# Memory keys and values moved into the MLP, and the norms and first blocks of the second stage cut into token halves

## The chip, the cores and the metric

The kernel runs on one core of a Trainium2 chip. The metric is the device time of one execution in microseconds (us); smaller is better. Matrix products run on TensorE (PE), elementwise work on VectorE (DVE) and ScalarE (ACT), small fills on GpSimd (POOL), and SyncE (SP) issues the transfers. Each engine works through its own list of instructions strictly in order, and waits on semaphores for what the others have made.

## The reference

One sequence of 1,024 tokens, 1,024 features, goes through two stages. The first is a residual block with a gated long convolution, a recurrent branch, a mix of both, and an MLP:

```
h = rms_norm(x, g_mlp); f = square(relu(h @ w_1)); x = x + f @ w_2
return rms_norm(x, g_final)
```

The second stage normalises that result again, projects it, and adds three branches to it. Of them the change touches the beginning of two and the memory's side of the third:

```
mn = rmsnorm(mem, mem_norm_g); km, vm = split(mn @ w_kv)     # 256 memory rows
u -> sums over windows of 2, 4, 8, 16 tokens -> pool_w -> gate by zb
gates (8 columns) -> log-sigmoid, cumulative sum, cumulative maximum over the tokens
```

All is float32 in the reference.

## The kernel before, in words

**Products.** Every float32 operand of a large product is split into a high part and a low part, so that one product becomes three matmuls (`three_products`, L564 to L566). Activations lie feature-major, as 8 tiles of 128 features by 1,024 tokens; a weight block of 1,024 by 128 against one half of the tokens (512) is 8 x 3 = 24 matmuls, and a whole block has two such halves (`block`, `block_product`).

**Weights.** All weight blocks stand in one list, `blocks`, and pass through two raw buffers and three split buffers. SP loads block i once block i-2 has been split (`ahead`, L423); ACT makes the high part (L946) and DVE the low part (L1471), both once PE has used block i-3. Where in its list each engine does this is written out by hand, by calls of `ahead(k)`.

**PSUM.** Results go to banks that are handed out in a ring (`Rota`, L107). In the MLP the ring has six banks: who asks for a bank waits until the sixth request before it has been read out and freed. At the second stage the ring grows to eight.

**The end of the MLP.** The MLP runs in four quarters (f = 0 to 3). Of each, eight blocks `w1` make a quarter of f, and eight blocks `w2` are added to x (L1832). In the last quarter each finished tile of x is squared by ACT (`stat_square`, L1186), and DVE adds it into two running sums (L1799, L1800): one of the squares and one of the squares times the squared gain, from which both norms, one after the other, are computed. Memory is loaded and normalised there too.

**After the MLP.** PE turns the normalised memory feature-major (L749), DVE and ACT split it (L955, L1486), and four key blocks (24 matmuls of 256 columns) and four value blocks (12 matmuls of 512 columns) follow. Within them PE sums the running sums over the features by one-column matmuls (L730), DVE computes both norms' factors (L1870 to L1882), PE spreads the factors over the partitions (L605), and h3, the input of the second stage, is scaled by DVE (L1861) and split by ACT and DVE (L955, L1483). Then `y1_start` (L1890) makes x into the first norm's result, 16 instructions.

**The second stage's start.** Blocks `gates`, then for each of four groups `u`, `zb` and `pw`, then the four blocks `ob`. DVE computes on the gate rows (4 partitions by 1,024 tokens) cumulative sums (L1896 to L1905) and maxima (L1906 to L1919); PE transposes one of these rows (L791). For each group DVE sums windows over u (L1949 to L1958), ACT and DVE split the result, `pw` multiplies it, and it is gated (L1922, L1975). `ob` needs all four groups.

Of the kernel before, what the change touches and what calls it, by code (L numbers as in the profile page):

```python
# [9 lines left out]
P = 128  # L10
# [109 lines left out]
def build_program(nc, A, out):  # L120
    ctx = ExitStack()
    with ctx:
# [102 lines left out]
        for j in range(DT):  # L225
            need(("wo", j), w_o, 0, DT, j * P, P)
        for f in range(FC):
            for j in range(DT):
                need(("w1", f, j), w_1, 0, DT, (f * DT + j) * P, P)
            for j in range(DT):  # L230
                need(("w2", f, j), w_2, f * D, DT, j * P, P)
        for c in range(NH):
            need(("kv", c), w_kv, 0, DT, c * P, P)
        for c in range(NH):
            need(("kv", NH + c), w_kv, c * 2 * P, 2, GROUP, GROUP)
# [3 lines left out]
        for g in range(NH):  # L239
            need(("u", g), w_in2, 0, DT, Y_U + g * P, P)  # L240
            need(("zb", g), w_in2, 0, DT, Y_ZB + g * P, P)
            need(("pw", g), A["pool_w_2"][0, g], 0, 1, 0, P)
# [99 lines left out]
        sqm = [sb(f"sqm{n}", "g", 36 * KB + 4096 * n, [P, SEQ]) for n in range(2)]  # L342
        square_sum = [sb(f"square_sum{n}", "g", 44 * KB + 4096 * n, [P, SEQ]) for n in range(2)]
        tmp2 = [sb(f"tmp_2_{n}", "g", 72 * KB + 2048 * n, [P, HALF]) for n in range(4)]
# [4 lines left out]
        row = [sb(f"row{n}", "g", (8 + 17 + 8) * KB + 4096 * n, [P, SEQ]) for n in range(5)]  # L349
# [66 lines left out]
        def sync(sp):  # L416
# [81 lines left out]
            ahead(number["kv", 2 * NH - 1] + 2)  # L498
# [4 lines left out]
            ahead(number["gates"] + 2)  # L503
# [8 lines left out]
            sp.dma_start(rcnt[:], A["rcnt"]).then_inc(*landed("rcnt", ("rcnt",)))  # L512
# [38 lines left out]
        def tensor(pe):  # L551
# [174 lines left out]
            def stat_sums():  # L726
                w.wait_ge(*at("square_sums", DT - 1))
                for n in range(2):
                    for t in range(NT):
                        last = pe.matmul(stat_bank[:, n * NT + t:n * NT + t + 1], square_sum[n][:, t * P:(t + 1) * P], ones[:, 0:1],  # L730
                                         start=True, stop=True, skip_group_check=True)
                last.then_inc(*up("pe_done", ("stat",)))

            for f in range(FC):
# [5 lines left out]
                for j in range(DT):  # L740
                    for half in range(2):
                        block_product(number["w2", f, j], ("w2", f, j, half), ff, f"ff{f}", half, used=half == 1)

            for j in range(0, DT, 2):
                b = bank("mem", j)
                w.wait_ge(*at("mem_normed", 0))
                w.wait_ge(*at("mem_normed", 1))
                for q in range(4):
                    turned = pe.transpose(b[:, q * P:(q + 1) * P], mem_in[:, q % 2, (j + q // 2) * P:(j + q // 2 + 1) * P], ident[:])  # L749
                turned.then_inc(*up("pe_done", ("mem_turned", j)))  # L750
            for c in range(2 * NH):
                if c == 1:
                    stat_sums()
                    ring.names, ring.turn = ring.names + [("x1_var", 0), ("stat",)], 0
                if c == NH:
                    w.wait_ge(*at("r12"))
                    for half in range(2):
                        spread(8, half, "h3_scale")
                k = number["kv", c]
                hi, lo = weight_views(k)  # L760
                if c < NH:
                    b = bank("kv", c)
                elif c == NH:
                    value_banks = [bank("values", q) for q in range(NM)]
                w.wait_ge(*at("w", k))
                if c < NH:
                    for n in range(DT):
                        w.wait_ge(*at("mn_lo", n))
                        three_products(b[:, 0:N_MEM], (hi[:, n, :], lo[:, n, :]), (mn[0][n][:], mn[1][n][:]), n == 0,
                                       [("kv", c), ("used", k)] if n == DT - 1 else None)  # L770
                else:
                    for q in range(NM):
                        qs = slice(q * P, (q + 1) * P)
                        for n in range(2):
                            j = (c - NH) * 2 + n
                            point = ([("values", q)] if c == 2 * NH - 1 else []) + ([("kv", c), ("used", k)] if q else [])
                            three_products(value_banks[q][:], (mn[0][j][:, qs], mn[1][j][:, qs]), (hi[:, n, :], lo[:, n, :]), j == 0,
                                           point if n and point else None, stop=c == 2 * NH - 1)
            w.wait_ge(*at("r1"))
            for half in range(2):  # L780
                spread(0, half, "y1_scale")


            block(("gates",), h3, "h3")
            for g in range(NH):
                block(("u", g), h3, "h3")
                if g == 0:
                    b = bank("x_turn")
                    w.wait_ge(*at("x_row"))
                    for c in range(NT):  # L790
                        last = pe.transpose(b[:, c * NH:(c + 1) * NH], row[0][0:NH, c * P:(c + 1) * P], ident[0:NH, 0:NH])  # L791
                    last.then_inc(*up("pe_done", ("x_turned",)))
                block(("zb", g), h3, "h3")
                k = number["pw", g]
                hi, lo = weight_views(k)
                for half in range(2):
# [4 lines left out]
                                   [("pw", g, half)] + ([("used", k)] if half else []))  # L801
            for c4 in range(4):
                add_block(("ob", c4), yp, "yp", NH)
# [130 lines left out]
        def scalar(act):  # L934
# [247 lines left out]
            def stat_square(j):  # L1182
                w.wait_ge(*at("x2", j, 1))
                w.wait_ge(*(at("square_sums", j - 2) if j >= 2 else at("w1", FC - 1, DT - 1, 1)))
                to = sqm[j % 2] if j else square_sum[0]
                act.activation(to[:], x1[j][:], ACT.Square).then_inc(*did(("sqm", j)))  # L1186

            for f in range(FC):
# [13 lines left out]
                for j in range(DT):  # L1202
                    ahead(number["w2", f, j] + 2)
                    if f == FC - 1 and j:
                        stat_square(j - 1)
                    if f == FC - 1 and j in (1, 2):
                        w.wait_ge(*at("mem_in"))
                        w.wait_ge(*now("act_done"))
                        act.activation(mem_sq[:], mem_in[:, j - 1, :], ACT.Square, accum_out=stat[:, 15 + j:16 + j]).then_inc(
                            *did(("mem_square", j - 1)))  # L1210
                        root(slice(15 + j, 16 + j), f"mem{j - 1}")


            for j in range(0, DT, 2):
                for q in range(2):
                    w.wait_ge(*at("mem_turned", j))
                    if q:
# [994 lines left out]
```

## Time and profile before

| | us |
|---|---|
| median of three runs | 2616.26 |
| the runs | 2615.48 to 2619.42 |
| the profiled execution's own time | 2618.09 |
| its span | 2616.3 |
| PE busy / share | 2490.5 / 95% |
| DVE busy / share | 1394.7 / 53% |
| ACT busy / share | 823.1 / 31% |

The profiled execution stands 1.8 us above the median. The granted TensorE clock over it is 0.979 of full speed. The page's slices of 65 us show PE busy at nine tenths nearly everywhere, with a few slices at eight tenths; one of these lies where the MLP ends and the second stage begins, and PEclk dips there too.

### The profile page before, as it was taken

To read this page: it belongs to the slowest core of one execution; us is meant where nothing else is said; L and a number is where in the kernel's file an instruction comes from. 1 tells how busy PE (TensorE), PEld (TensorE's weight loads), DVE (VectorE), ACT (ScalarE), POOL (GpSimd) and SP (SyncE) were. 2 spreads that over 40 slices of the span, in tenths; PEclk is the share of its full clock that TensorE was granted. 3 is DMA by queue.
4 is the path that set the end of the run, shared out by engine and by line. 5 is a ranking of instruction groups with operands and counts; after the bars stand their busy time and mean duration, and the time that the engine had idled before them with its cause. 6 is when DMAs were issued, how large, how long until landed. Compare 5 with 4: busy or idle time off the path is not lost.

```text
span 2616.3 us, 26218 instructions
## 1 busy us (share of the span) xinstructions
PE 2490.5 (95%) x11144; PEld 2013.6 (77%) x11144; DVE 1394.7 (53%) x1657; ACT 823.1 (31%) x1224; POOL 2.8 (0%) x7
## 2 busy tenths in 40 slices
PE   8999999999898999999999999998889999999678
PEld 6778677786785788888888888887778777878577
DVE  5588798888884734343232332334655333631365
ACT  5342533425121613332131220222322231221354
POOL 0000000000000000000000000000000000000000
PEclk9999999999999999999999999999899999999889
DMA  4102112021210112211111111111111111111401
GB/s 135 45 21 66 40 52 66 15 75 35 98 49 16 41 49 80 82 41 56 41 49 56 42 56 49 44 62 49 42 52 58 33 33 49 41 49 56 129 24 57
DMA packets 226679, 139.44 MB, mean 53 GB/s; under 512 B 12922, under 2 KB 221050, under 8 KB 226562
## 3 DMA queue, kind: packets, MB, share of 16 engines
q1 hardware_dynamic: 226562, 137.76, 17.9%
q8 instruction: 88, 1.44, 0.2%
q14 instruction: 29, 0.24, 0.0%
HBM read 128.27 MB, written 9.47 MB: 53 GB/s over the span
## 4 chain that ended last, share of the span: by engine, by line
PE 79%; DVE 12%; ACT 6%; issue 1%; DMA 1%; SPq 1%; DVEq 0%; ACTq 0%
PE bank L564 24%; PE bank L566 24%; PE bank L565 24%; DVE acc L1596 3%; DVE lru L1575 1%; PE bank L598 1%; PE bank L628 1%; DVE wlo L1471 1%; DVE lru L1565 1%; PE bank L813 1%; DVE lru L1577 1%; DVE lru L1573 1%; PE bank L829 1%; PE bank L721 1%; DVE lru L1568 1%
## 5 line engine op out<-in xcount | busy, mean ns | idle before, releaser
L564 PE MATMUL bank<-h_hi,whi 128*128 128x512 f32 x2000 | 789.6, 395 | 8.1 <-DVE wlo L1471 4.7
L566 PE MATMUL bank<-h_hi,wlo 128*128 128x512 f32 x2000 | 780.9, 390 | 0.0
L565 PE MATMUL bank<-h_lo,whi 128*128 128x512 f32 x2000 | 780.7, 390 | 0.0
L564 PEld LDWEIGHTS bank<-h_hi,whi 128*128 128x128 f32 x2000 | 377.0, 188 | 91.3 <-issue 12.7
L565 PEld LDWEIGHTS bank<-h_lo,whi 128*128 128x128 f32 x2000 | 377.0, 189 | 81.3 <-issue 3.9
L566 PEld LDWEIGHTS bank<-h_hi,wlo 128*128 128x128 f32 x2000 | 376.7, 188 | 78.7
L946 ACT ACTIVATE whi<-raw 128x1024 fp32r<-128x1024 f32 (+2 forms) x212 | 216.7, 1023 | 476.4 <-PE bank L566 458.2
L1471 DVE TENSOR_TENSOR wlo<-raw,whi 128x1024 fp32r<-128x1024 f32 (+2 forms) x212 | 251.1, 1185 | 199.7 <-ACT whi L946 198.2
L1596 DVE SCALAR_TENSOR_TENSOR acc<-u_in,par,acc 128x1024 f32<-128x1024 f32 x240 | 308.3, 1285 | 8.2
L566 PE MATMUL bank<-ff_hi,wlo 128*128 128x512 f32 x512 | 199.4, 389 | 0.0
L564 PE MATMUL bank<-ff_hi,whi 128*128 128x512 f32 x512 | 199.3, 389 | 0.0
L565 PE MATMUL bank<-ff_lo,whi 128*128 128x512 f32 x512 | 199.3, 389 | 0.0
L1832 DVE TENSOR_TENSOR x<-x,bank 128x512 f32<-128x512 f32 x64 | 44.0, 688 | 229.8 <-PE bank L566 229.8
L1198 ACT ACTIVATE tmp<-tmp 128x512 f32<-128x512 f32 x64 | 40.5, 632 | 227.4 <-DVE tmp L1821 227.4
L566 PEld LDWEIGHTS bank<-ff_hi,wlo 128*128 128x128 f32 x512 | 96.1, 188 | 19.9
L565 PEld LDWEIGHTS bank<-ff_lo,whi 128*128 128x128 f32 x512 | 96.1, 188 | 19.9
L564 PEld LDWEIGHTS bank<-ff_hi,whi 128*128 128x128 f32 x512 | 96.1, 188 | 19.9
L1821 DVE SCALAR_TENSOR_TENSOR tmp<-bank,factor 128x512 f32<-128x512 f32 x64 | 44.2, 691 | 115.9 <-PE bank L566 115.9
L628 PE MATMUL bank<-v,gate_w 128*128 128x512 f32 x224 | 98.3, 594 | 1.8 <-DVE lru L1565 1.8
L1483 DVE TENSOR_TENSOR ff_lo<-tmp,ff_hi 128x512 fp32r<-128x512 f32 x64 | 44.3, 692 | 87.2 <-ACT ff_hi L955 87.2
L628 PEld LDWEIGHTS bank<-v,gate_w 128*128 128x128 f32 x224 | 42.3, 190 | 53.2 <-issue 46.1
L564 PE MATMUL bank<-vg_hi,whi 128*128 128x512 f32 x192 | 77.2, 402 | 5.8 <-DVE yb L1635 5.8
(342 smaller groups left out, 2952.3 us busy)
## 6 DMA issues: line engine op xcount, KB each, us to landing
raw<-in_w_in SPq DMA_DIRECT2D x92, 512.0 KB, 3.7
raw<-in_w SPq DMA_DIRECT2D x64, 512.0 KB, 3.8
raw<-in_w_b_out SPq DMA_DIRECT2D x16, 384.0 KB, 3.1
raw<-in_w_out SPq DMA_DIRECT2D x11, 512.0 KB, 3.4
x_in<-in_x SPq DMA_DIRECT2D x8, 512.0 KB, 6.0
raw<-in_w_a_out SPq DMA_DIRECT2D x8, 512.0 KB, 3.9
raw<-in_w_o SPq DMA_DIRECT2D x8, 512.0 KB, 3.7
xcols<-in_x SPq DMA_DIRECT2D x16, 256.0 KB, 2.8
```

The costliest lines, as they stand in the source:

```text
L564: pe.matmul(target, lh, rh, start=start, stop=False, skip_group_check=True)
L565: pe.matmul(target, lh, rl, start=False, stop=False, skip_group_check=True)
L566: last = pe.matmul(target, ll, rh, start=False, stop=stop and point is not None, skip_group_check=True)
L598: pe.matmul(b[:], ones_sq[:], data, start=j == 0, stop=j == DT - 1, skip_group_check=True).then_inc(*up("pe_done", point))
L628: last = pe.matmul(b[:], gate_w[n][:, PAIRS.index((a, c)), :], v[a][:, cut(half)], start=m == 0, stop=m == len(rows_) - 1)
L946: act.activation(hi, raw_, ACT.Copy).then_inc(*up("w_hi_done", ("w_hi", i)))
L1198: act.activation(t[:], t[:], ACT.Square).then_inc(*did(("relu_square", f, j, half)))
L1471: dve.tensor_tensor(lo, raw_, hi.bitcast(F32), ALU.subtract).then_inc(*up("w_lo_done", ("w", i)))
L1483: dve.tensor_tensor(lo, value, hi.bitcast(F32), ALU.subtract).then_inc(*did(name, *more))
L1596: dve.scalar_tensor_tensor(to[:], source, weight, to[:], ALU.mult, ALU.add).then_inc(*did(*([("uc", j)] if m == TAPS_A - 1 else [])))
L1821: dve.scalar_tensor_tensor(t[:], b[:], 0.0, factor[:, cut(half)], ALU.max, ALU.mult).then_inc(*did(("relu", f, j, half), ("free", "w1", f, ...
L1832: dve.tensor_tensor(x1[j][:, cut(half)], x1[j][:, cut(half)], b[:], ALU.add).then_inc(*did(("x1_add", f, j, half), ("free", "w2", f, j, ha ...
```

## The change

It does five things.

1. The blocks of keys and values go into the last quarter's `w2` blocks: keys 0 and 1 before block 5, keys 2 and 3 and the four values before blocks 6 and 7. Memory is transposed after blocks 2 and 3, and its tiles are split by ACT and DVE in their lists after blocks 3 and 4.
2. The last two `w2` blocks run as (6, first half), (7, first half), (6, second half), (7, second half), and squares, sums, one-column matmuls and norm factors go by halves of the tokens.
3. h3 is made half by half, with the low part of a tile issued after the scaling of the next one (`h3_low`).
4. `gates`, `u0` and `u1` are multiplied tile by tile as h3 comes: `gates` and `u0` together for the first half, `u1` alone, then all three for the second half (`tiles_together`).
5. The gate rows' work and `y1_start` go later in DVE's list: cumulative sums and half of `y1_start` in group 0, the other half in group 1, the maxima in group 2. `y1_start` reads its factor from SBUF. The transposed row is made just before `ob`. The counts for short windows (`rcnt`) are loaded with memory.

```
+        KV_AT = {5: (0, 1), 6: tuple(range(2, 2 * NH))}
...
+            for j in range(DT - 2):                        # VectorE
+                ahead(number["w2", FC - 1, j] + 2)
                 for half in range(2):
+                    x2_tile(FC - 1, j, half)
+                if j:
                     for half in range(2):
+                        square_sums(j - 1, half)
...
+                if j in (3, 4):
+                    for m in range(4 * j - 12, 4 * j - 8):
+                        memory_tile(m)
...
+            for j in (DT - 2, DT - 1):
+                x2_tile(FC - 1, j, 0)
+                square_sums(j, 0)
+            means(0)
+            second_means(0)
+            factors(0)
+            w.wait_ge(*at("kv", 2 * NH - 1))
...
+            x2_tile(FC - 1, DT - 2, 1)
+            ahead(number["w2", FC - 1, DT - 2] + 3)
+            square_sums(DT - 2, 1)
+            x2_tile(FC - 1, DT - 1, 1)
+            square_sums(DT - 1, 1)
+            ahead(number["w2", FC - 1, DT - 1] + 3)
+            h3_part(0, 0, 1, 2, 3, 4)
+            means(1)
+            h3_part(0, 5)
+            second_means(1)
+            h3_part(0, 6)
+            factors(1)
+            h3_part(0, 7)
+            h3_low()
+            h3_part(1, *range(DT))
+            h3_low()
...
+            ahead(number["gates"] + 3)
+            ahead(number["u", 0] + 3)
+            pooled(0)
+            for g in range(NH):
+                ahead(number["zb", g] + 2)
+                zb_tile(g)
+                if g + 1 < NH:
+                    pooled(g + 1)
+                ahead(number["pw", g] + 2)
+                yp_tile(g)
+                if g + 2 < NH:
+                    ahead(number["u", g + 2] + 2)
+                if g == 0:
+                    gate_sums()
+                if g < 2:
+                    for first in (0, 4):
+                        y1_start(g, first)
+                if g == 2:
+                    gate_maxima()
```

```
+                for j in range(DT if f < FC - 1 else DT - 2):   # TensorE
+                    if f == FC - 1:
+                        for c in KV_AT.get(j, ()):
+                            key_block(c)
+                    block(("w2", f, j), ff, f"ff{f}")
+                    if f == FC - 1 and j in (2, 3):
+                        turn_memory(4 * j - 8)
+                        turn_memory(4 * j - 6)
...
+            for j in (DT - 2, DT - 1):
+                block_product(number["w2", FC - 1, j], ("w2", FC - 1, j, 0), ff, f"ff{FC - 1}", 0, used=False)
+            block_product(number["w2", FC - 1, DT - 2], ("w2", FC - 1, DT - 2, 1), ff, f"ff{FC - 1}", 1)
+            stat_sums(0)
+            block_product(number["w2", FC - 1, DT - 1], ("w2", FC - 1, DT - 1, 1), ff, f"ff{FC - 1}", 1)
+            w.wait_ge(*at("r12", 0))
+            spread(8, 0, "h3_scale")
...
+            tiles_together([("gates",), ("u", 0)], 0, h3, "h3", lambda: stat_sums(1))
+            ring.names, ring.turn = ring.names + [("x1_var", 0), ("stat", 1)], 6
+            block_product(number["u", 1], ("u", 1, 0), h3, "h3", 0, used=False)
+            w.wait_ge(*at("r12", 1))
+            spread(8, 1, "h3_scale")
             for half in range(2):
                 spread(0, half, "y1_scale")
+            tiles_together([("gates",), ("u", 0), ("u", 1)], 1, h3, "h3")
...
+            for g in range(NH):
+                block(("zb", g), h3, "h3")
+                pool_product(g)
+                if g + 2 < NH:
+                    block(("u", g + 2), h3, "h3")
```

```
+            def memory_tile(m):                            # ScalarE
+                w.wait_ge(*at("mem_turned", m // 2 * 2))
+                if m % 2:
+                    w.wait_ge(*at("mn_lo", m - 1))
+                split_hi(("mn_hi", m), ...)
...
+            def memory_tile(m):                            # VectorE; frees the bank of a pair
+                w.wait_ge(*at("mn_hi", m))
+                scaled_lo(("mn_lo", m), ..., *([("free", "mem", m - 1)] if m % 2 else []))
...
+            gate_rows(1)
+            u_tile(0, 1)
+            ahead(number["gates"] + 3)
```

## Rows read from the trace of the kernel before

**Rows 1.** The page, part 4: the chain that ended last, by engine.
```profile
PE 79%; DVE 12%; ACT 6%; issue 1%; DMA 1%; SPq 1%; DVEq 0%; ACTq 0%
```

**Rows 2.** Stretches: PE, PEld, DVE, ACT, POOL busy us; then granted clock, DMA share, GB/s.
```profile
1750.00:1800.00 50.00, 50.00 (x222) 41.41 (x221) 23.79 (x29) 11.38 (x14) 0.00 (x0) 1.00 0.18 53
1860.00:1870.00 10.00, 4.92 (x14) 3.54 (x13) 6.97 (x10) 3.46 (x5) 0.00 (x0) 0.66 0.20 52
1812.00:1999.00 187.00, 158.12 (x714) 132.51 (x713) 115.45 (x154) 62.59 (x93) 0.95 (x1) 0.89 0.17 47
```

**Rows 3.** Waits of TensorE, 1795 to 2000 us: total us, times, longest.
```profile
PE bank L564 <- DVE wlo L1471: 8.6, 2, 5.1
PE bank L791 <- DVE row L1905: 8.4, 1, 8.4
```

**Rows 4.** Timeline of TensorE: start, length, instruction, idle time before it and releaser.
```profile
1813.73 1.91 PE L749 MATMUL bank<-ident,mem_in 128*128 128x128 f32 x16
...
1827.37 6.99 PE L730 MATMUL bank<-ones,square_sum 128*128 128x1 f32 x32 [3.87 <-DVE square_sum L1800]
...
1865.50 0.79 PE L564 MATMUL bank<-whi,mn_hi 128*128 128x512 f32 x1 [5.08 <-DVE wlo L1471]
...
1869.74 0.40 PE L565 MATMUL bank<-wlo,mn_hi 128*128 128x512 f32 x1
...
1997.25 0.50 PE L564 MATMUL bank<-yp_hi,whi 128*128 128x512 f32 x1 [1.55 <-DVE yp_lo L1483]
```

**Rows 5.** Timeline of VectorE, the MLP's end, memory and norm factors.
```profile
1808.48 0.69 DVE L1832 TENSOR_TENSOR x<-x,bank 128x512 f32<-128x512 f32 x1 [1.09 <-PE bank L566]
...
1813.93 0.69 DVE L1832 TENSOR_TENSOR x<-x,bank 128x512 f32<-128x512 f32 x1 [4.76 <-PE bank L566]
...
1822.34 0.48 DVE L1486 SCALAR_TENSOR_TENSOR mn_lo<-bank,par,mn_hi 128x256 fp32r<-128x256 f32 x1 [0.54 <-ACT mn_hi L955]
...
1834.39 0.17 DVE L1870 COPY stat<-bank 128x16 f32<-128x16 f32 x1 [7.08 <-PE bank L730]
...
1836.37 0.17 DVE L1882 TENSOR_TENSOR stat<-stat 128x8 f32<-128x8 f32 x1
```

**Rows 6.** Timeline of VectorE, scaling and splitting of h3, a weight's low part.
```profile
1846.02 0.75 DVE L1861 SCALAR_TENSOR_TENSOR tmp<-x,small,bank 128x512 f32<-128x512 f32 x1 [1.18 <-PE bank L605]
1847.46 0.69 DVE L1483 TENSOR_TENSOR h_lo<-tmp,h_hi 128x512 fp32r<-128x512 f32 x1 [0.70 <-ACT h_hi L955]
...
1849.51 0.69 DVE L1483 TENSOR_TENSOR h_lo<-tmp,h_hi 128x512 fp32r<-128x512 f32 x1 [0.70 <-ACT h_hi L955]
...
1864.22 1.23 DVE L1471 TENSOR_TENSOR wlo<-raw,whi 128x1024 fp32r<-128x1024 f32 x1 [0.25 <-ACT whi L946]
```

**Rows 7.** Timeline of VectorE, y1_start, gate rows, the last group's windows.
```profile
1884.70 10.62 DVE L1890 SCALAR_TENSOR_TENSOR x<-x,par,bank 128x512 f32<-128x512 f32 x16
...
1896.37 1.21 DVE L1896 SCALAR_TENSOR_TENSOR row<-row 4x1024 f32<-4x1024 f32 x1
...
1907.21 0.91 DVE L1906 MEMSET row<- 4x1024 f32 x1 [0.16 <-issue]
...
1913.42 0.12 DVE L1938 MEMSET uw<- 128x16 f32 x3
...
1982.09 5.05 DVE L1949 TENSOR_TENSOR uw<-uw 128x1039 f32<-128x1039 f32 x4 [5.76 <-ACT uw L1265]
...
1990.88 1.22 DVE L1471 TENSOR_TENSOR wlo<-raw,whi 128x1024 fp32r<-128x1024 f32 x1
```

**Rows 8.** Timeline of ScalarE: two keys copied out, a gate row.
```profile
1842.25 0.38 ACT L1238 ACTIVATE km<-bank 128x256 f32<-128x256 f32 x1 [1.55 <-PE bank L566]
...
1845.12 0.38 ACT L1238 ACTIVATE km<-bank 128x256 f32<-128x256 f32 x1 [1.55 <-PE bank L566]
...
1885.33 0.67 ACT L1249 ACTIVATE row<-bank,small 4x512 f32<-4x512 f32 x1
```

**Rows 9.** Transfers issued from 1770 to 1900 us: size, median us to landing.
```profile
raw<-in_w_mem_kv SPq DMA_DIRECT2D x8, 512.0 KB, 3.5
```

More of the change, by code:

```diff
@@ L751, in tensor @@
[L751 to L778, printed above, removed]
@@ new lines, in tensor, with tiles_together @@
+            spread(8, 0, "h3_scale")
+            def tiles_together(keys, half, right, right_name, middle=None):
+                together = [bank(*key, half) for key in keys]
+                for n in range(DT):
+                    w.wait_ge(*at(f"{right_name}_lo", n, half))
+                    for key, b in zip(keys, together):
+                        k = number[key]
+                        hi, lo = weight_views(k)
+                        w.wait_ge(*at("w", k))
+                        point = [(*key, half)] + ([("used", k)] if half else []) if n == DT - 1 else None
+                        three_products(b[:], (hi[:, n, :], lo[:, n, :]), (right[0][n][:, cut(half)], right[1][n][:, cut(half)]), n == 0,
+                                       point)
+                    if middle and n == 3:
+                        middle()
@@ L1207, in scalar @@
                         w.wait_ge(*at("mem_in"))
                         w.wait_ge(*now("act_done"))
[L1209 to L1217, printed above, removed]
-                        w.wait_ge(*at("mn_lo", j))
-                    split_hi(("mn_hi", j + q), mn[0][j + q][:], bank("mem", j)[:, q * N_MEM:(q + 1) * N_MEM], C("mem_norm_g_2", j + q))
@@ new lines, in scalar, with h3_part @@
+            km_tile(0)
+            km_tile(1)
+            for half in range(2):
+                stat_square(DT - 3, half)
+            for c in range(2, 2 * NH):
+                ahead(number["kv", c] + 2)
+                if c < NH:
+                    km_tile(c)
+            for q in range(NM):
+                w.wait_ge(*at("values", q))
+                act.activation(vm[:, q, :], bank("values", q)[:], ACT.Copy).then_inc(*did(("vm", q), ("free", "values", q)))
+            def h3_part(half, *tiles):
+                for j in tiles:
@@ new lines, in vector, with means @@
+            for half in range(2):
+                square_sums(DT - 3, half)
+            for c in range(2, 2 * NH):
+                ahead(number["kv", c] + 2)
+            columns = lambda n, half: slice(8 * n + 4 * half, 8 * n + 4 * half + 4)
+            def means(half):
+                w.wait_ge(*at("stat", half))
+                both_ = stat[:, 0:2 * NT].rearrange("p (n t) -> p n t", n=2)[:, :, 4 * half:4 * half + 4]
+                dve.tensor_copy(both_, stat_bank[:, 0:2 * NT].rearrange("p (n t) -> p n t", n=2)[:, :, 4 * half:4 * half + 4]).then_inc(
+                    *did(("free", "stat", half)))
+                own()
+                mean(columns(0, half), f"r1_{half}")
@@ L1886, in vector @@
-            for half in range(2):
-                b = bank("y1_scale", half)
-                w.wait_ge(*at("y1_scale", half))
-                for j in range(DT):
-                    dve.scalar_tensor_tensor(y1[j][:, cut(half)], x1[j][:, cut(half)], C("g_final", j), b[:], ALU.mult,
-                                             ALU.mult).then_inc(*did(("y1_start", j, half), *([("free", "y1_scale", half)] if j == DT - 1 else [])))
-            ahead(number["gates"] + 2)
-            w.wait_ge(*at("f_row"))
```

409 lines of the change are left out of this document (237 added, 172 removed).

## The prediction, made before the changed kernel was run

> **What bounds the kernel now.** I read the page's chain first: 79% of it is TensorE [rows 1], so only PE's idle or slowed time can be won. The stretches come next. Inside the MLP PE is busy all the time at clock 1.00; from 1812 to 1999 it is busy 158 of 187 us at a mean clock of 0.89 [rows 2]. The waits and PE's timeline name the gaps: two weight splits (8.6 us) and the gate row (8.4) [rows 3], the square sums (3.87) [rows 4], and smaller ones.
>
> I compare from the end of the last `w2` block (PE free at 1813.73) to PE's wait for the last `yp_lo` inside `ob` (1997.25) [rows 4]: 183.5 us. The MLP's last quarter before it and everything behind keep their order, but for transfers that land early enough.
>
> Work in it at full clock. A half block takes 5.44 us, the distance of two x additions [rows 5], so one 512-column matmul 0.227. A key block takes 2.87 [rows 8], memory's 16 transposes 1.9, a transpose-like matmul 0.12 [rows 4]. Nine blocks 97.9, four `pw` 5.4, keys 11.5, values 10.9, memory 1.9, spreads 3.9, gate row 1.0, `ob`'s first nine matmuls 2.0, and one-column sums 32 x 0.12 = 3.8 (they ran in 6.99 at the low clock [rows 4]; I take half). Sum 138.4. So 45.1 us are stall or low clock. The change leaves the work as it is; what counts is the stalls it leaves or makes. I walk through each engine's new list with the durations of the rows.
>
> **Unit costs.** An add waiting for PE starts 0.20 behind it [rows 4, 5]. Half-width DVE instructions follow each other every 0.61 (tensor_tensor, 0.69 long) or 0.66 (16 in 10.62 [rows 7]). From ScalarE's start on a weight to PE 2.36: 1.08, then 1.28 from 1864.22 to 1865.50 [rows 4, 6]. A transfer 3.5 to 3.7 [rows 9]. Clock: after 5.08 idle, ten matmuls took 4.24 us instead of 2.27 [rows 4], and the stretch reads 0.66 [rows 2]: the lower of the two levels, 1.2 GHz, for a while; a loss of about 2 per gap of some length, and none behind the 1.55 gap at 1997.25 [rows 4].
>
> **Part 1, memory, keys and values inside the MLP.** Transposes go after block 2, but in DVE's list the memory tiles stand behind both x additions of block 3, and the ring has six banks: block 4's first half asks for the bank of the first memory pair. That is free only when DVE has done, from block 3's end: 0.20, add and own wait 0.79, four half-width sums 2.7, two memory tiles 1.5 (0.48 + 0.54 for ScalarE + 0.48 [rows 5]): 5.2. PE has 0.96 of transposes to fill it: **stall 4.25, clock 1.8**. Bounds: 0 if the bank were free, 6.
>
> Key 0 follows block 4 at once but needs memory tiles 4 to 7, behind block 4's additions and sums in the same list: tile 4 is there 4.2 after block 4's end, tile 7 2.4 later; the key ends at 7.0 instead of 2.9: **4.1, clock 0.7**. Value 0's weight is split behind x additions and eight sums of blocks 4 and 5 (6.2 + 0.2 + 1.28 against 5.8 of keys): **1.9**. Then raw buffers: block i's load waits for split i-2, 3.3 to 3.7 landing, 2.36 to PE, against 2.7 of work per value: **0.2** and, for `w2` 6, **0.6**. Together 13.6, and the last `w2` half ends at 1813.73 + 26.2 (memory, keys, values, half of the one-column sums) + 13.6 = 1853.6. Call this T.
>
> **Part 2, halves of the norm and h3.** DVE stands at `means(0)` until the one-column sums of half 0, at T-5.4; factors 2.15 (1834.39 to the end of 1836.37 [rows 5]); then memsets, add for block 6, two weight low parts, two sums: it reaches block 7's last add at T+1.2, not T+0.2. Square and sums to T+3.9, low part of `u1` to T+5.0, first scaling. The first low part starts 1.44 after it [rows 6] and PE 0.75 later: T+7.2. PE has 1.0 of spread: **6.3, clock 2.0**. The low part needs 1.27 per tile in the new order (0.66 + 0.61; before 2.05 [rows 6]), PE uses 1.36 per tile, so it keeps up. In the middle `means(1)` waits for PE's sums and holds back tile 4 by 2.0; tiles 5 to 7 come late by the small factor instructions: **3.4** together. Gates and `u0`, half 0, end at T+25.4; `u1` at 30.9; h3's second half starts 3.3 later: **0.35**. Three blocks' second halves 16.3: T+50.4.
>
> **Part 3, `zb0`.** Its buffer is free when `gates` ends, 1.4 before. ScalarE has in front of it two gate rows (0.7 each [rows 8]) and a `u` copy (0.5), then 2.36: **3.1, clock 1.7**. The buffers are three and three blocks are in use, so no other cover exists. `zb0` ends at T+66.2.
>
> **Part 4, DVE's list sets PE.** From `zb0`'s end DVE does in order: gate 0.8 + 0.6; windows of group 1; low part of `zb1` 1.1; products and splits of group 0, 4.1 (2 x 2.05); `gate_sums` 10.7 (1896.37 to 1907.21 less its gap [rows 7]), 1.4 after that because the gate row's copy stands behind `u2`'s on ScalarE; half of `y1_start` 5.3; and only then the low part of `u3`. Windows: group 3 took 8.8, of which 1.27 per add [rows 7], so group 1 takes 6.3, group 2 7.5. PE can start `u3` at T+98.0; it was done with `pw1` at 90.6: **7.4, clock 2.6**. After it, `zb2` ends at T+122.4; DVE: gate 1.4, windows of group 3 8.8, 0.3, products of group 2 4.1, maxima 6.2 (1907.21 to 1913.42 [rows 7]), then the low part of `ob0` (1.1, T+143.3), gate 1.3, `ob1` 1.1, and `yp_lo` 2.2 later at PE: T+149.1. PE would have been there at T+139.1: **10.0**.
>
> The Trainium skill, "VectorE: DVE Perf Modes", section on the TRN2 errata, gives PSUM-sourced VectorE work 120 fixed cycles and SBUF-sourced 58. `y1_start` moves to SBUF; the eight on the path would be an estimated 0.5 us shorter. The rows' 0.69 for an SBUF pair against 0.74 to 0.75 with PSUM says 0.4. I leave either out.
>
> **Sum.** New stalls 6.05 + 4.8 + 1.9 + 0.8 + 8.3 + 3.4 + 0.35 + 4.8 + 10.0 + 10.0 = 50.4, old 45.1: **+5.3**. The other way: 1853.6 + 149.1 = 2002.7 against 1997.25, +5.4. On the profiled execution's own time, 2618.1 becomes 2623.4; the median lies 1.8 below it, so I say 2621.5.
>
> So the old waits (splits, square sums, gate row) go, but each comes back behind another instruction of the same DVE: memory tiles, `u1`'s split, `gate_sums` before `u3`, maxima before `ob0`.
>
> **Rivals.** A, faster: the memory tiles don't hold PE. If the bank is free and the tiles are ready when block 4 and key 0 ask, 6.05 + 4.8 go: -5.5, 2610.7. For it: PE is never idle in the MLP now [rows 2]. Against: six banks and the order in DVE's list. It decides from the point where the first memory pair is read out within 1 us of block 3's end.
> B, same: the clock does not fall in the new gaps. Terms 1.8, 0.7, 2.0, 1.7 and 2.6 fall away: -3.5, 2612.7. Against: rows 4 show it behind 5.08 idle.
> C, slower still: the one-column sums let the clock fall. In the old order all 32 ran at the low level [rows 4]; if each half does here, it is 1.6 more plus about 1.7 behind it, twice: +12, 2628.
> D, the change does what the numbers of PE alone say, and everything is covered: -45. DVE's own list of about 85 us against PE's 71 behind `gates` rules it out; I give it nothing.
>
> The Trainium skill, "TensorE: Matmul & The Clock Gate", part 1, says that the number of slow matmuls at a start differs from run to run (6, 11 or 14). The ten of rows 4 lie between. By that a clock term could be an estimated 0.8 less or more, which changes no sign.
>
> **How the numbers follow.** A difference of under 0.2% (5.2 us) can't be told from none here, and my sum lies on that line. Forecast 0.50, own range 2616 to 2627, a little over half of it slower. A 0.13, of which 0.10 faster; B 0.17, all same; C 0.20, slower. Slower 0.27 + 0.20 = 0.47; faster 0.12 with something for an overlap that I missed; same 0.41. Range 2611 to 2630: down to A, up past C; bounds of the unmeasured terms (bank 0 to 6, clocks 0 to 9) lie inside it.
>
> **What would show it.** PE idle some 4 us before `w2` 4 with VectorE `mn_lo` as releaser; again inside key 0; some 6 us before the first h3 matmul; 7 us before `u3`, released by a weight's low part right behind `y1_start`; 7 before `ob0`, behind the maxima. Wrong would be PE busy without a gap before 1840, or `u3` without a wait. If the total is faster, look first at the memory tiles.

## The result, and the profile after

The changed kernel takes 2627.03 us, the median of six runs (2625.16 to 2629.02); the kernel before, beside it on the same chip, 2617.08 (2615.48 to 2622.13). The ratio is 1.0033, 95% interval 1.0023 to 1.0044: slower, about 9 us, clear of the 0.2% that can be told here. The profiled spans say the same, 2624.8 against 2616.3. The forecast was 2621.5 in a range of 2611 to 2630: inside, and the rise of 5.3 us that it named is some 3 to 5 us short of the measured one. The forecast gave slower a chance of 0.47 and same one of 0.41, so the right sign was little better than an even chance.

The chain of the changed kernel has the same shares as before [rows 1]:

```profile
PE 79%; DVE 12%; ACT 6%; issue 1%; DMA 1%; SPq 1%; DVEq 0%; ACTq 0%
```

So it doesn't show the change at this resolution. The stretches do. The columns are those of [rows 2]. The first three are of the changed kernel, in the MLP's last quarter, behind it up to `ob` (a stretch shifted with the work), and from the first memory transpose to the wait for the last `yp_lo`.

```profile
1750.00:1800.00 50.00, 42.69 (x202) 35.79 (x201) 24.75 (x40) 11.73 (x21) 0.00 (x0) 0.93 0.13 38
1812.00:2007.00 195.00, 165.96 (x730) 135.97 (x729) 119.42 (x169) 62.70 (x91) 0.96 (x1) 0.91 0.16 45
1759.46:2004.70 245.24, 208.89 (x939) 172.20 (x937) 140.52 (x199) 74.07 (x111) 0.96 (x1) 0.92 0.16 43
```

The kernel before, over the same work (from the end of `w2` block 2's last matmul to the last `yp_lo` wait of [rows 4]):

```profile
1759.33:1997.25 237.92, 209.04 (x938) 174.70 (x937) 140.05 (x181) 71.62 (x102) 0.95 (x1) 0.91 0.17 47
```

This pair is the result in two lines. TensorE is busy 208.89 us instead of 209.04: same matmuls, and the same time spent in them, low clock included. The stretch grew by 7.32, and PE's idle time in it from 28.88 to 36.35, by 7.47. The MLP's last quarter was full before (50.00 of 50.00 in [rows 2]) and is 42.69 of 50.00 now. Another 0.7 us comes right behind the stretch: the first matmul on the keys with the query of the following stage starts at 2058.87, where before it started at 2050.69, so +8.2 there.

Who holds TensorE: waits of the changed kernel from 1720 to 2020, in the columns of [rows 3].

```profile
PE bank L575 <- DVE wlo L1566: 20.9, 5, 8.0
PE bank L575 <- DVE mn_lo L1581: 7.3, 3, 4.2
PE bank L575 <- ACT h_hi L1000: 5.7, 1, 5.7
PE bank L575 <- DVE h_lo L1578: 2.2, 2, 1.7
PE bank L575 <- DVE yp_lo L1578: 0.2, 1, 0.2
```

The gate row (8.4) and the two long weight splits of [rows 3] and the square sums of [rows 4] are gone from the list. In their place stand mostly low parts of other weights. Those before value 0, `u3` and `ob0` (2.09, 7.30 and 7.98 us) wait only for their turn in VectorE's list; those before `zb0` and `w2` 6 (3.08 and 0.43) wait for ScalarE's high part. The TensorE timeline shows where (columns of [rows 4]):

```profile
1776.53 0.50 PE L575 MATMUL bank<-ff_hi,whi 128*128 128x512 f32 x1 [4.24 <-DVE mn_lo L1581]
...
1793.41 0.39 PE L575 MATMUL bank<-mn_hi,whi 128*128 128x256 f32 x1 [2.66 <-DVE mn_lo L1581]
...
1819.08 0.47 PE L575 MATMUL bank<-whi,mn_hi 128*128 128x512 f32 x1 [2.09 <-DVE wlo L1566]
...
1847.28 1.84 PE L741 MATMUL bank<-ones,square_sum 128*128 128x1 f32 x16
...
1854.57 1.05 PE L616 MATMUL bank<-ident,stat 128*128 128x128 f32 x8
...
1861.36 0.77 PE L575 MATMUL bank<-h_hi,whi 128*128 128x512 f32 x1 [5.74 <-ACT h_hi L1000]
...
1872.82 0.51 PE L575 MATMUL bank<-h_hi,whi 128*128 128x512 f32 x1 [1.71 <-DVE h_lo L1578]
...
1908.44 0.80 PE L575 MATMUL bank<-h_hi,whi 128*128 128x512 f32 x1 [3.08 <-DVE wlo L1566]
...
1954.04 0.77 PE L575 MATMUL bank<-h_hi,whi 128*128 128x512 f32 x1 [7.30 <-DVE wlo L1566]
...
2000.31 0.79 PE L575 MATMUL bank<-yp_hi,whi 128*128 128x512 f32 x1 [7.98 <-DVE wlo L1566]
2004.70 0.80 PE L575 MATMUL bank<-yp_hi,whi 128*128 128x512 f32 x1 [0.18 <-DVE yp_lo L1578]
```

In order: `w2` block 4, key 0, value 0, the end of the MLP (T = 1854.57), the first matmul on h3, the late fifth tile of h3's first half, `zb0`, `u3`, `ob0` and `ob1`. The 16 one-column sums take 1.84 us, 0.115 each; the 32 of before took 6.99 [rows 4].

VectorE's timeline of the changed kernel gives the reason for three of the four largest waits (4.24, 7.30 and 7.98 us):

```profile
1774.31 0.74 DVE L1896 SCALAR_TENSOR_TENSOR square_sum<-sqm,gcol,square_sum 128x512 f32<-128x512 f32 x1
1774.97 0.48 DVE L1581 SCALAR_TENSOR_TENSOR mn_lo<-bank,par,mn_hi 128x256 fp32r<-128x256 f32 x1
1775.99 0.88 DVE L1581 SCALAR_TENSOR_TENSOR mn_lo<-bank,par,mn_hi 128x256 fp32r<-128x256 f32 x2 [0.54 <-ACT mn_hi L1000]
...
1936.78 1.21 DVE L2045 SCALAR_TENSOR_TENSOR row<-row 4x1024 f32<-4x1024 f32 x1 [1.36 <-ACT row L1373]
1941.48 1.22 DVE L2047 SCALAR_TENSOR_TENSOR row<-row,row 4x1024 f32<-4x1024 f32 x1 [3.50 <-ACT row L1377]
...
1947.39 5.37 DVE L2039 SCALAR_TENSOR_TENSOR x<-x,par,y_row 128x512 f32<-128x512 f32 x8
1952.69 1.21 DVE L1566 TENSOR_TENSOR wlo<-raw,whi 128x1024 fp32r<-128x1024 f32 x1
...
1992.86 0.91 DVE L2057 MEMSET row<- 4x1024 f32 x1
...
1999.05 1.21 DVE L1566 TENSOR_TENSOR wlo<-raw,whi 128x1024 fp32r<-128x1024 f32 x1
```

The memory tile that frees block 4's bank runs right behind block 3's square sums; the low part of `u3` (1952.69) right behind `gate_sums` and half of `y1_start`; that of `ob0` (1999.05) right behind the maxima. What VectorE does first is needed by nobody soon. It is not busy in all of that time: of the 10.6 us that `gate_sums` takes from 1936.78 to 1947.39, VectorE waits 3.50 for ScalarE, which makes the logarithm of the row in between, and 1.36 more before them. The list holds back the weight split through these waits too. The fourth wait, 5.74 us before the first matmul on h3, hangs on the same list: VectorE scales h3's first tile only at 1859.13, behind block 7's addition, its sums and `u1`'s low part, and ScalarE waits for that.

For `zb0` it is ScalarE's list. VectorE is idle there and waits for the high part, which stands behind two gate rows and a copy of `u`:

```profile
1905.45 0.60 ACT L1322 ACTIVATE uw<-bank 128x512 f32<-128x512 f32 x1
1906.07 1.26 ACT L991 ACTIVATE whi<-raw 128x1024 fp32r<-128x1024 f32 x2
...
1907.16 1.43 DVE L1566 TENSOR_TENSOR wlo<-raw,whi 128x1024 fp32r<-128x1024 f32 x2 [10.15 <-ACT whi L991]
```

### The profile page after: what moved, and what is told of

It is laid out like the page before. It is cut to its first block, busy times and chain, and to the rows that moved or that the text cites. A ratio compares the mean times of both kernels' runs of the same rounds, so it can differ in the third digit from the quotient of the medians.

```text
span 2624.8 us, 26255 instructions
## 1 busy us (share of the span) xinstructions
PE 2493.0 (95%) x11144; PEld 2013.0 (77%) x11144; DVE 1397.1 (53%) x1682; ACT 826.3 (31%) x1236; POOL 2.8 (0%) x7
## 4 chain that ended last, share of the span: by engine, by line
PE 79%; DVE 12%; ACT 6%; issue 1%; DMA 1%; SPq 1%; DVEq 0%; ACTq 0%
PE bank L575 24%; PE bank L576 24%; PE bank L577 24%; DVE acc L1691 3%; DVE lru L1670 1%; PE bank L609 1%; DVE wlo L1566 1%; PE bank L639 1%; DVE lru L1660 1%; PE bank L858 1%; DVE lru L1668 1%; DVE lru L1672 1%; PE bank L874 1%; PE bank L732 1%; DVE lru L1663 1%
```

## The experiments

Each kernel was timed four to eleven times beside the kernel before, and profiled once. Ratios are to the kernel before; the changed one stands at 1.0033. Every experiment but the last starts from the changed kernel. To locate a gain I compare the starts of one and the same instruction, the first keys-by-query matmul (2058.87 in the changed kernel), and take off how much earlier or later the unchanged part ahead of the stretch ended: that part moved by up to 2.5 us from profile to profile. The slowest and the fastest execution of one kernel lie 3 to 9 us apart, so a gain read from two profiles is located well, but its size is good to a few microseconds only.

**Memory tiles first.** This tries the forecast's account of the stalls inside the MLP against the idea that TensorE would wait there for something else.

```
 ahead(number["w2", FC - 1, j] + 2)
+if j in (3, 4):
+    for m in range(4 * j - 12, 4 * j - 8):
+        memory_tile(m)
 for half in range(2): x2_tile(FC - 1, j, half)
 if j:
     for half in range(2): square_sums(j - 1, half)
-if j in (3, 4):
-    for m in range(4 * j - 12, 4 * j - 8):
-        memory_tile(m)
```

> The changed kernel with one move: in VectorE's list the memory tiles stand ahead of the x additions and sums of blocks 3 and 4, not behind them. Theory W (the waits of the walk are made by the order of VectorE's list): the bank wait (4.24 us), the waits in key 0 (2.66 + 0.41) and the slow matmuls behind both (about 1.8 and 1.3) go, some 11 us; the span falls from 2624.8 to about 2613.5, and w2 block 5 starts 11 us earlier. Rival R1 (the memory tiles cannot be made in time wherever they stand, because transposes, splits and six banks are too tight together): PE still idles 3 us or more there, span 2621 or above.

Measured: median 2617.72, ratio 0.9989 (0.9980 to 0.9998), span 2614.3; the common instruction starts at 2048.31, 10.6 earlier, 10.3 without the part ahead. Both waits are gone, and the next one is value 0's weight:

```profile
1807.41 0.47 PE L575 MATMUL bank<-whi,mn_hi 128*128 128x512 f32 x1 [2.09 <-DVE wlo L1566]
1807.71 0.39 PE L576 MATMUL bank<-wlo,mn_hi 128*128 128x512 f32 x1
1807.94 0.53 PE L577 MATMUL bank<-whi,mn_lo 128*128 128x512 f32 x1
1808.26 0.63 PE L575 MATMUL bank<-whi,mn_hi 128*128 128x512 f32 x1
```

The place of eight small VectorE instructions (and of ScalarE's halves of them, which follow) was worth the whole loss of the change. The rival is refuted. A by-product: this 2.09 us gap is as long as the changed kernel's at 1819.08, but here eight matmuls behind it take 0.53 to 0.63 instead of 0.39.

**Gate rows' work late.** The sums go behind `ob` block 0's additions, the maxima behind block 1's, with what belongs to them on the other engines.

```
 for g in ...:
-    if g == 0: gate_sums()          # VectorE, before u3's split
-    if g == 2: gate_maxima()        # before ob0's split
 # behind the additions of one ob block:
+    if key == "ob" and c4 == 0: gate_sums()
+    if key == "ob" and c4 == 1: gate_maxima()
+    if key == "ob" and c4 == 2: (copy of x_turn)
 # PE: x_turn behind ob block 2; ScalarE: the f row in ob block 0;
 # SyncE: ahead(number["ob", 3]) before it waits for the m row
```

> The changed kernel with the gate rows' work (sums, maxima, ScalarE's part, the transposed row) moved behind the first blocks of ob; SP loads three weight blocks further before it waits for the maxima. Theory W (from zb0's end VectorE's list is longer than PE's work, and gate_sums and maxima are what PE waits for): the waits before u3 (7.30) and ob0 (7.98) go but for about 2.5, with the slow matmuls behind u3; the wait for the last yp_lo comes about 16 us earlier (2004.7 to about 1989), and nothing is given back inside ob, so span about 2608.5. Rival R2 (the gate work is only moved; VectorE then holds up ob's additions and the banks): the time comes back inside ob, span 2617 or more.

Measured: median 2609.86, ratio 0.9961 (0.9949 to 0.9974), span 2612.8; the common instruction at 2046.95, 11.9 earlier; the part ahead of the stretch ran 1.84 later, so 13.8 inside (16 expected). `u3` waits for nothing, `ob0` for 2.5 in place of 8:

```profile
1986.62 0.50 PE L575 MATMUL bank<-yp_hi,whi 128*128 128x512 f32 x1 [2.49 <-DVE wlo L1567]
1991.00 0.80 PE L575 MATMUL bank<-yp_hi,whi 128*128 128x512 f32 x1 [1.18 <-DVE yp_lo L1579]
```

The missing 2 us are a second wait (2.49 + 1.18 us against 2.5 expected) and a low clock from 1987.91 on, twelve matmuls, eight of them behind the last wait. I had not expected it behind a gap of 2.5. This profile is the slowest of the kernel's five executions; by the ratios (0.9961 against 1.0033) the gain is some 19 us, with an interval of 4 to either side. What makes the other four faster, at a mean granted clock of 0.982 to 0.984 against the profile's 0.979, is not shown. The rival, that the 10.7 + 6.2 us of work would merely hold the `ob` blocks instead, is refuted: they run behind the last thing that TensorE needs soon.

**Only `u3` early.** If VectorE has more in its list than TensorE, freeing one split moves the wait to the next.

```
 if g == 0:
+    ahead(number["zb", 1] + 2)      # VectorE and ScalarE: u3's weight is split first
     gate_sums()
```

> The changed kernel with only u3's weight split moved ahead of gate_sums on ScalarE and VectorE. Theory W (VectorE's whole list bounds, so a wait removed at u3 comes back at zb2): PE starts u3 without a wait, then idles about 6.4 us before zb2; the wait for the last yp_lo moves by 0.8 us, span about 2624. Rival R3 (the wait before u3 is local, a badly placed split): 7.3 + 2.2 us won, span about 2615.

Measured: median 2624.76, ratio 1.0018 (1.0010 to 1.0027), span 2623.8; the common instruction 1.8 earlier. The 7.30 at `u3` are gone, and 6.24 of them come back one block later:

```profile
1963.67 0.76 PE L575 MATMUL bank<-h_hi,whi 128*128 128x512 f32 x1 [6.24 <-DVE wlo L1567]
...
1999.25 0.80 PE L575 MATMUL bank<-yp_hi,whi 128*128 128x512 f32 x1 [7.98 <-DVE wlo L1567]
```

This is the forecast's Part 4 ("DVE's list sets PE") shown directly: one wait of 7.3 removed, 1.8 won. Of the 1.8, 1.06 is the wait's difference and 0.7 is three slowed matmuls behind `ob1` that this profile does not have. By the ratios it is 4 us, with 4 to either side; the 9.5 of rival R3 lie outside that. Only taking work off the list ahead of `ob0`, as the experiment before does, wins it.

**`zb0`'s split first.**

```
-gate_rows(1); u_tile(0, 1)
 ahead(number["gates"] + 3)
+gate_rows(1); u_tile(0, 1)
```

> The changed kernel with zb0's and pw0's weight splits ahead of the two gate rows and the u copy on ScalarE. Theory W (two gate rows and the copy, 1.9 us, stand in front of the split): the wait before zb0 falls from 3.08 to about 1.2 us. If the clock does not fall behind so short a gap (none fell behind 1.55 in the kernel before), another 2.9 us are won: span about 2620. Rival R4 (the clock has no price of its own here): 1.9 us, span about 2623. Rival R5 (the split waits for the buffer, not for ScalarE): nothing, 2624.8.

Measured: median 2624.36, ratio 1.0011 (1.0002 to 1.0020), span 2623.4. Inside the stretch 3.1 us are won (the common instruction, less the part ahead, which ran 2.16 later). That is less than my account expected, for a reason that the timeline shows:

```profile
1908.97 0.50 PE L575 MATMUL bank<-h_hi,whi 128*128 128x512 f32 x1 [1.11 <-DVE wlo L1566]
...
1915.86 0.50 PE L575 MATMUL bank<-h_hi,whi 128*128 128x512 f32 x1 [1.11 <-ACT uw L1322]
```

The first wait falls from 3.08 to 1.11 and no matmul is slow behind it (13 were). But `u_tile(0, 1)`, now later on ScalarE, reads out the bank that `zb0`'s second half asks for: a new 1.11. So rival R5 fell (the split does not wait for the buffer), and R4 too (thirteen slowed matmuls went with the gap). The bank ring is a constraint of the same kind as the list, and I had it only for memory's tiles.

**Gaps filled.** In front of five waiting matmuls (`w2` 4, h3, `zb0`, `u3`, `ob0`) TensorE runs 17, 24, 12, 30 and 32 matmuls whose results nobody reads.

```
+def fill(b, left, right, n):
+    for _ in range(n):
+        pe.matmul(b[:], left, right, start=True, stop=True, skip_group_check=True)
 # before the wait for the weight or bank, in block_product and at h3:
+fill(...)
```

> The changed kernel with PE kept busy in five of its gaps by matmuls of stable tiles into a bank that nobody reads (17 before w2 block 4, 24 before the first h3 matmul, 12 before zb0, 30 before u3, 32 before ob0); no wait is taken away. Theory W with the clock's price: no slow matmuls behind these gaps any more (counts 8, 11, 13, 10 and 12 in the changed kernel's trace, about 0.2 us each and 0.35 at each first), every wait is as long as before, and the span falls by 9 to 10 us, to about 2615. Rival B of the prediction (the fallen clock has no price of its own, since other waits take its place): span within 2 us of 2624.8.

Measured: median 2619.59, ratio 1.0003 (0.9994 to 1.0012), span 2617.8, 7.0 less than the changed kernel's, 7.8 inside the stretch. The same work waits just as long for VectorE, but TensorE runs at full clock afterwards. So the low clock behind those five gaps costs about 8 us, and rival B's premise ("the clock does not fall") is refuted. The 7.8 are net: behind the two gaps that stay open before the values, more matmuls ran slow than in the changed kernel, 27 of 256 columns behind key 0's 2.66 (18 there) and eight of 512 behind value 0's 2.09 (none there), together some 2.8 us:

```profile
1818.69 0.47 PE L575 MATMUL bank<-whi,mn_hi 128*128 128x512 f32 x1 [2.09 <-DVE wlo L1581]
...
1819.73 0.63 PE L575 MATMUL bank<-whi,mn_hi 128*128 128x512 f32 x1
...
1949.46 0.50 PE L575 MATMUL bank<-h_hi,whi 128*128 128x512 f32 x1 [0.41 <-DVE wlo L1581]
...
1993.69 0.50 PE L575 MATMUL bank<-yp_hi,whi 128*128 128x512 f32 x1 [0.48 <-DVE wlo L1581]
...
1998.06 0.50 PE L575 MATMUL bank<-yp_hi,whi 128*128 128x512 f32 x1 [2.04 <-DVE yp_lo L1593]
```

The last two lines show one place where rival B is right. In the changed kernel nine slowed matmuls stand between the starts of `ob0` and `ob1`, 4.39 us apart; here the nine run at full speed, and the starts are 4.37 apart, because TensorE now waits 2.04 for the last `yp_lo`. A low clock that ends in a wait for another engine costs nothing. Behind the 2.04 gap no matmul is slow (granted clock 1.00 from 1998 to 2006).

**The three repairs together**, and the bank of the h3 scale's second half requested ahead of `u1`'s first half, which turns the ring so that `zb0`'s second half no longer asks for that bank.

```
 # the edits of memory tiles first, gate rows late, zb0's split first, and:
+scale_bank = bank("h3_scale", 1)
 block_product(number["u", 1], ("u", 1, 0), h3, "h3", 0, used=False)
-spread(8, 1, "h3_scale")
+spread(8, 1, "h3_scale", scale_bank)
```

> The changed kernel with the three moves of e1, e2 and e4 together, and the bank of h3_scale (second half) asked for before that of u1's first half, so that zb0's second half does not wait for u's copy. Theory W (each wait is local to its place, so the gains add): e1 gave 10.3, e2 13.8, e4 3.1 and the new bank wait of e4 1.1, sum 28.3, span about 2596.5. Rival R6 (VectorE's list is full, so the gains overlap): 2605 or more.

Measured: median 2596.84, ratio 0.9913 (0.9900 to 0.9927), span 2595.9. The common instruction starts at 2030.06, 28.8 earlier, although the part ahead ran some 1.7 later: about 30.5 inside. The three alone and the 1.11 of the ring make 10.3 + 13.8 + 3.1 + 1.1 = 28.3; the rest is the low clock behind the 2.49 gap at `ob0`, which this profile doesn't have. The costs add up in the profiles, so they are separate, and R6 (2605 or more) is refuted. By the ratios the three single gains make 36 us and this version's is 31, a difference of 5 with an interval of 8 to either side: they agree, but less sharply than the profiles.

```profile
1897.87 0.50 PE L575 MATMUL bank<-h_hi,whi 128*128 128x512 f32 x1 [1.11 <-DVE wlo L1568]
...
1971.42 0.50 PE L575 MATMUL bank<-yp_hi,whi 128*128 128x512 f32 x1 [2.49 <-DVE wlo L1568]
```

**And the two that are left.** Value 0's weight is split ahead of the sums of blocks 4 and 5; the `gates` weight and block 6's addition go ahead of the norm's factors, and `square_sums(7, 1)` and `u1`'s split behind the first h3 tiles.

```
+ahead(number["kv", 2] + 2)                    # VectorE and ScalarE
 square_sums(DT - 3, 0); square_sums(DT - 3, 1)
 ...
+ahead(number["gates"]); x2_tile(FC - 1, DT - 2, 1)
 means(0); second_means(0); factors(0)
 ...
 x2_tile(FC - 1, DT - 1, 1)
-x2_tile(FC - 1, DT - 2, 1)                    # stood behind factors(0)
-square_sums(DT - 1, 1)
-ahead(number["w2", FC - 1, DT - 1] + 3)
-h3_part(0, 0, 1, 2, 3, 4)
+h3_part(0, 0, 1, 2, 3)
+square_sums(DT - 1, 1)
+h3_part(0, 4)
+ahead(number["w2", FC - 1, DT - 1] + 3)
```

> e6 with two further moves in the lists of VectorE and ScalarE: the first value block's split ahead of the sums of blocks 4 and 5, and at the end of the MLP gates' split and block 6's addition ahead of the first norm factors, the squares' last sums and u1's split behind the first h3 tiles. Theory W: the 2.09 us wait before the values and its slow matmuls (1.6) go; the first h3 matmul comes 3.5 us earlier, the gap before it falls from 5.7 to about 2.2; span about 2589.5, 7 below e6. Rival R7 (the one-column sums of the second half come later and give that back): within 2 us of e6 plus the 3.7 of the values.

Measured: median 2588.62, ratio 0.9877 (0.9864 to 0.9891), span 2583.2. This is the fastest version of the study, 32 us under the kernel before. Inside the stretch it wins 7.8 on the version above (7 expected); 4.2 more of the profile's difference lie ahead of the stretch, where nothing was changed, and I don't count them (the medians differ by 8.2). R7, which allowed 5.7 at most, is refuted. Its waits from 1750 to 2010, its first h3 matmul, and its stretches:

```profile
PE bank L575 <- DVE wlo L1570: 3.8, 3, 2.5
PE bank L575 <- ACT h_hi L1002: 2.3, 1, 2.3
PE bank L575 <- DVE h_lo L1582: 2.2, 2, 1.7
PE bank L575 <- DVE yp_lo L1582: 2.0, 1, 2.0
```

```profile
1841.45 0.47 PE L575 MATMUL bank<-h_hi,whi 128*128 128x512 f32 x1 [2.27 <-ACT h_hi L1002]
```

```profile
1750.00:1800.00 50.00, 50.00 (x264) 43.02 (x263) 26.49 (x40) 15.67 (x27) 0.00 (x0) 1.00 0.21 64
1812.00:1966.00 154.00, 143.82 (x647) 118.44 (x646) 96.98 (x142) 51.39 (x79) 0.96 (x1) 0.98 0.17 47
```

36.3 us of waits have become 10.3, the quarter with memory and keys in it is full again, and the granted clock of the rest is 0.98 instead of 0.91.

**The old kernel with its gate rows late.** Does any of this need the change? Here the kernel before gets the second experiment's edit alone (with buffers moved so that the windows don't lie over the gate rows, and the counts `rcnt` loaded with memory).

```
 # kernel before; VectorE: its two steps as functions, called behind ob blocks
+    if key == "ob" and c4 == 0: gate_sums()
+    if key == "ob" and c4 == 1: gate_maxima()
-# both in one piece behind y1_start
```

> The kernel before, unchanged in its MLP, norms and blocks, with only the gate rows' sums, maxima and transposed row moved behind the first blocks of ob (the rows' and scratch tiles' places in SBUF as in the changed kernel). Theory W (in the old order too VectorE's gate rows are a local wait): the 8.37 us before the transposed row, 2.6 of slow matmuls and the 0.74 wait behind them go, span about 2604.8 against 2616.3. So e6 minus this, some 8 us, would be what token halves and the moved memory are worth. Rival R8 (the old order's gates overlap with h3 and y1_start, and the wait comes back at yp_lo): span above 2611.

Measured: median 2607.09, ratio 0.9948 (0.9935 to 0.9962), span 2607.1; the common instruction 11.2 earlier, 12.2 without the part ahead. R8 (span above 2611) is refuted. The gate row's 8.37 are gone; the old waits for values and square sums stay:

```profile
1866.66 0.80 PE L564 MATMUL bank<-whi,mn_hi 128*128 128x512 f32 x1 [5.04 <-DVE wlo L1469]
...
1985.21 0.50 PE L564 MATMUL bank<-yp_hi,whi 128*128 128x512 f32 x1 [1.55 <-DVE yp_lo L1481]
```

So of what the repaired version wins, 0.52% is there without the change. The rest, 0.9913 / 0.9948 = 0.9965 or about 9 us, and 0.9877 / 0.9948 = 0.9929 or about 19 us with the last edits, is what the repaired versions win beyond that, with some 5 us of uncertainty on either figure.

It is not shown that all of this is owed to moved memory and token halves. The old kernel got one repair, the new one up to five. The old kernel's waits of 3.49 and 5.04 us for value weights are of the same kind: in its profile the splits of these weights stand in the lists of ScalarE and VectorE behind four tiles of h3 each. Nobody tried to put them earlier there. If that worked, the 9 and 19 us would shrink by those waits and the slowed matmuls behind them, so they are upper bounds.

## Why the prediction was right, and where its sizes were off

The forecast said that each old wait would go and come back behind another instruction of the same VectorE, for +5.3. It did, for +7.3 in the stretch and +8.2 with what follows. By its steps, idle time first, then matmuls at the low clock. I call a matmul slowed when the next one starts 0.43 us behind it instead of 0.23, or 0.21 instead of 0.12 for a key's; where eight of them run, from 1873.0 to 1876.5, the granted clock reads 0.53, so it is at the lower of its two levels (1.2 GHz of 2.4) for nearly all of that time. So one of 512 columns loses 0.2 us and one of a key's 0.1. The counts are from the timeline:

- `w2` 4's bank, 4.25 + 1.8: 4.24, and 8 slowed matmuls, 1.6. Right to a hundredth of a microsecond, as was the reason (ring and order of the list): the first experiment takes it away.
- Key 0, 4.1 + 0.7: 2.66 + 0.41, and 18 slowed key matmuls, 2.0. Idle is 1 us less than priced, clock 1.3 more.
- Value 0's weight, 1.9: 2.09. Raw buffers, 0.8: 0.43.
- T, 1853.6: 1854.57.
- First h3 matmul, 6.3 + 2.0: 5.74, and 11 slowed matmuls, 2.2.
- Middle of the halves, 3.4 + 0.35, with no clock term: 1.71 + 0.53, and 8 slowed matmuls, 1.6. This is clock that I left out: it comes behind 1.84 us of one-column sums and then 1.71 idle.
- `zb0`, 3.1 + 1.7: 3.08, and 13 slowed matmuls, 2.6.
- `u3`, 7.4 + 2.6 at T + 98.0: 7.30, 10 slowed matmuls, 2.0, at T + 99.5.
- `ob0` and `ob1`, 10.0: 7.98 + 0.18, and 9 slowed matmuls between the two, 2.0, which stand where a wait for `yp_lo` would stand otherwise (see the filled gaps). Three more behind it make the 0.7 past the end of my sum, which compared the kernels at the last `yp_lo` wait; the kernel before had a 1.55 gap there and no slowed matmul behind it [rows 4].

Waiting was forecast as 41.6 (with all of `ob0`'s 10.0 in it) and is 36.35; low clock was forecast as 8.8 and is 14.0 by these counts (16.1 if everything above the 192.8 us of work at full clock is called so: the forecast's 138.4 and five `w2` blocks of 10.88). So the working was too dear by 5 on waiting and too cheap by 7 on the clock, of which 2 at `ob0` are one and the same time under two names. The rest of the two errors cancelled, which is luck; 2.0 is what remains. The mis-sized term is the clock: I gave it 0.7 to 2.6 behind five gaps and nothing in the middle and behind `ob0`; it came behind seven. It is no reason why the changed kernel is slower, though: by the same reckoning the kernel before spends 16.2 us of its stretch at the low clock, and the whole rise is idle time.

The Trainium skill, "TensorE: Matmul & The Clock Gate", part 1, lets the number of slowed matmuls at a kernel's start differ from run to run. The traces agree for gaps in the middle: behind one and the same wait of 4.24 us before `w2` 4 there are 8 in the changed kernel and 10 with the gate rows late, and behind 2.09 us none (changed kernel) or eight (the first experiment). But this is not what made the clock term too small: that is key 0, priced at 0.7 and measured at 2.0, `zb0`, priced at 1.7 and measured at 2.6, and the two places without a term.

The Trainium skill, "VectorE: DVE Perf Modes", section on the TRN2 errata, would have eight `y1_start` instructions from SBUF an estimated 0.5 us shorter. The trace does not agree: eight took 5.37 us from SBUF, sixteen 10.62 from PSUM [rows 7], 0.67 and 0.66 each. Leaving it out was right. The forecast's own 0.4 from rows was a misreading: it compared two operations. A `tensor_tensor` takes 0.69 with a PSUM operand too [rows 5], and a `scalar_tensor_tensor` 0.74 from SBUF alone (1774.31 above).

Rivals. A: TensorE was idle 4.24 and 2.66 at the memory tiles, so it fell; with the tiles placed first the 10.85 of its two terms are won nearly whole (10.3). B: fell, since filled gaps won 7.8, except between `ob0` and `ob1`, where it holds. C: the one-column sums of each half ran at full clock, 16 in 1.84, and no low clock came behind them where no gap followed; where a 1.71 gap followed it did. D: idle time grew. The five signs named in advance (4 before `w2` 4, again in key 0, 6 before h3, 7 before `u3` behind `y1_start`, 7 before `ob0` behind the maxima) all stand in the timeline.

Left open: why the part ahead of the stretch, the same code, ends up to 2.5 us earlier or 2.2 later from profile to profile; and how much of the last 9 to 19 us the old kernel would win with its value weights split earlier.

## What to carry to other kernels

Before moving work to where an engine is free, walk through the in-order list of the engine that feeds it, and ask of each instruction who waits for the one behind it: here eight memory tiles a few instructions too late, and 17 us of gate work too early, made the change a loss of 9 us; put right, it is a gain of 9 to 19 over an old kernel with the same gate work late and nothing else repaired. A wait that is removed without shortening the list ahead of the next one comes back there (7.3 removed, 1.8 won), and it pays to place long work of no urgency behind the last instruction that the bounding engine needs soon. Price every gap of more than 2.5 us on TensorE twice, as idle time and as about 2 us of low clock behind it (between 2 and 2.5 the second came only at times), and take the second price off where TensorE waits for the same engine again right after.

## What the runs showed of the hardware

- Gaps on TensorE of 0.2 to 1.55 us at full clock, between wide matmuls, had no slowed matmul behind them; 2.66 and more always had; between 2.04 and 2.49 it went either way: 2.04 without (gaps filled), 2.09 without (changed kernel) and with eight (memory tiles first), 2.27 with eight (the fastest version), 2.49 with twelve (gate rows late) and with none (the three repairs).
- 1.71 us of idle time behind 1.84 us of one-column sums had slowed matmuls behind it in each profile of the changed kernel and its variants, mostly eight. That the sums are the reason is likely but not shown: no gap between 1.55 and 2.04 us behind wide matmuls occurred.
- A one-column matmul takes 0.115 us at full clock and 0.218 at the low one (16 in 1.84 at a granted clock of 1.00; 32 in 6.99 [rows 4] at 0.50): it follows the clock like the wide ones.
- Filling five gaps with unread matmuls is worth 7 to 8 us here, net of the two gaps left open before the values, which had more slowed matmuls behind them than in the changed kernel.
- A low clock between two waits for the same engine cost nothing: `ob0` to `ob1` took 4.39 us with nine slowed matmuls and 4.37 with none.
